# The S5 state scan, run by VectorE within the heads of the gated recurrence instead of by GpSimd beside them

## What is computed

```python
def even_mixer(h_ctx, h_lat, ...):
    u, gs, xr, gr = split_proj(h)                        # S5 input, S5 gate, recurrence input, its gate
    ys_c, ys_l = prefix_bidir(s5_scan, (grp(u_c),), (grp(u_l),), s5p(0), s5p(1))
    yr_c, yr_l = prefix_bidir(rglru_scan, (centred_dwconv(xr_c, conv_w, conv_b),),
                              (centred_dwconv(xr_l, conv_w, conv_b),), rgp(0), rgp(1))

def rglru_scan(xc, wa, ba, wx, bx, lam):
    r = sigmoid(einsum(xh, wa) + ba); ig = sigmoid(einsum(xh, wx) + bx)
    log_a = -RG_C * r * softplus(-lam)
    h[t] = exp(log_a)[t] * h[t-1] + sqrt(-expm1(2 * log_a))[t] * (ig * xf)[t]
```

## Time and profile before

| | us |
|---|---|
| median of 3 runs | 3262.89 (3262.03 to 3270.83) |
| the profiled execution | 3270.08 |
| its span, first to last instruction | 3268.5 |
| TensorE busy in the span | 2768.8 (85%) |
| VectorE busy | 1510.1 (46%) |
| ScalarE busy | 759.5 (23%) |
| GpSimd busy | 1093.3 (33%) |

### The profile page before, as it was taken

One profiled execution on the slowest core, in us unless ns is written; L12 is line 12 of the kernel. 1 busy time (PEld: TensorE's weight loads), 2 busy tenths in 40 slices (PEclk: granted clock), 3 DMA queues, 4 the chain that ended last, 5 costly groups with the idle time before them and its releaser, 6 DMA issues. The chain is left out here.

```text
span 3268.5 us, 36705 instructions
## 1 busy us (share of the span) xinstructions
PE 2768.8 (85%) x13087; PEld 2137.8 (65%) x13087; DVE 1510.1 (46%) x1800; ACT 759.5 (23%) x906; POOL 1093.3 (33%) x1187
## 2 busy tenths in 40 slices
PE   7993556898896799798996999996598888989888
PEld 6652444444443577687884788885587878878777
DVE  2207996354455222243324655555645444544611
ACT  1210222224224111222212211112223223232211
POOL 0003886888888200001112433341232313232000
PEclk8796777998998799799998999998799999999999
DMA  4510122010110655524103233333102131213332
GB/s 144 170 66 28 64 73 80 20 48 26 35 42 13 205 185 182 169 79 170 33 27 80 101 117 117 125 122 125 46 23 101 55 104 37 101 43 97 123 103 65
DMA packets 256396, 289.29 MB, mean 89 GB/s; under 512 B 34688, under 2 KB 222376, under 8 KB 255920
## 3 DMA queue, kind: packets, MB, share of 16 engines
q1 hardware_dynamic: 200800, 198.36, 19.3%
q10 hardware_dynamic: 50672, 72.89, 6.2%
q0 software_dynamic: 4832, 16.78, 1.5%
HBM read 194.70 MB, written 93.29 MB: 88 GB/s over the span
## 5 line engine op out<-in xcount | busy, mean ns | idle before, releaser
L130 PE MATMUL ps<-arena,weights 128*128 128x512 f32 (+2 forms) x2432 | 762.3, 503 | 76.9 <-ACT arena L1195 64.6
L130 PEld LDWEIGHTS ps<-arena,weights 128*128 128x128 f32 (+1 forms) x2432 | 404.7, 180 | 423.1 <-issue 323.1
L130 PE MATMUL ps<-h_part,in_weight_parts 128*128 128x512 f32 (+1 forms) x1920 | 407.8, 373 | 14.0 <-DVE h_part L1513 7.8
L130 PEld LDWEIGHTS ps<-h_part,in_weight_parts 128*128 128x128 f32 x1920 | 334.7, 189 | 81.9 <-DVE h_part L1513 9.7
L130 PE MATMUL ps<-v_part,p_part 128*128 128x512 f32 x1248 | 300.0, 400 | 0.0
L130 PE MATMUL ps<-q_part,xc_part 128*128 128x256 f32 x1920 | 252.2, 296 | 38.2 <-DVE q_part L2014 36.0
L130 PEld LDWEIGHTS ps<-q_part,xc_part 128*128 128x128 f32 x1920 | 247.8, 204 | 41.9 <-DVE q_part L2014 38.5
L130 PEld LDWEIGHTS ps<-v_part,p_part 128*128 128x128 f32 x1248 | 238.2, 193 | 49.7
L1067 PE MATMUL ps<-wo_part,mx_part 128*128 128x512 f32 x768 | 178.7, 394 | 11.3 <-DVE mx_part L1963 8.3
L2248 POOL TENSOR_TENSOR in_weight_parts<-weights,ones 128x1024 fp32r<-128x1024 f32 x32 | 77.6, 2425 | 304.7 <-PE ps L130 231.5
L1067 PEld LDWEIGHTS ps<-wo_part,mx_part 128*128 128x128 f32 x768 | 145.0, 190 | 41.9 <-issue 8.5
(11 more groups left out here) (341 smaller groups left out, 3961.2 us busy)
## 6 DMA issues: line engine op xcount, KB each, us to landing
weights<-in_e_w_in SPq DMA_DIRECT2D x32, 512.0 KB, 4.3
weights<-in_o_w_in SPq DMA_DIRECT2D x32, 512.0 KB, 4.3
arena<-in_mod_w POOLq DMA_DIRECT2D x30, 512.0 KB, 5.5
s_out_maps<-arena ACTq DMA_DIRECT2D x16, 640.0 KB, 3.0
arena<-s_out_maps SPq DMA_DIRECT2D x16, 640.0 KB, 4.5
ml_xcv<-arena ACTq DMA_DIRECT2D x16, 640.0 KB, 5.1
xm_tiles<-ml_xm SPq DMA_DIRECT2D x16, 640.0 KB, 4.1
xc_full<-ml_xcv SPq DMA_DIRECT2D x4, 2560.0 KB, 10.6
```

The source lines that it names most:

```text
L130: return nc.tensor.matmul(o, lhsT, rhs, start=(k == 0), stop=(k == n - 1))
```

## The change

The loop on GpSimd is gone. VectorE clears `WZ[:, 0]` ahead of its loop over the heads, after waiting for `wz_a`, `wz_v` and `lam_ready` as GpSimd did, and runs the same four operations a step, 40 steps a head (SH = NJ // RH), unrolled in the loop's body: 8 ahead of the first tile's convolution, 4 ahead of the second's, 12 ahead of the two L1716, and 8 at the start of each direction. As the clearing now counts up `scan` too, those who wait for the whole scan wait for 4 * NJ + 1. The semaphore `scan0` is gone.

```diff
+            V.memset(WZ[:, 0], 0.0).then_inc(sem("scan"), 1)
+            n0, per, SH = link_n[0], 17, NJ // RH
             with dve.Fori(0, RH) as i:
+                k, step = [0], [0]
+                def scan_steps(n):
+                    for j in range(step[0], step[0] + n):
+                        z = WZ[:, bass.ds(SH * i + j, 1)].rearrange("p j r g -> p (j r) g")
+                        w = WZ[:, bass.ds(SH * i + (j + 1), 1)].rearrange("p j r g -> p (j r) g")
+                        dve.wait_ge(*past("scan", 4 * SH * i + (4 * j + 1)))
+                        V.tensor_tensor(SP1, z, A1, ALU.mult).then_inc(sem("scan"), 1)
+                        V.tensor_tensor(SP2[:, ::-1], z, A2, ALU.mult).then_inc(sem("scan"), 1)
+                        dve.wait_ge(*past("scan", 4 * SH * i + (4 * j + 3)))
+                        V.tensor_tensor(SP1, SP1, SP2, ALU.add).then_inc(sem("scan"), 1)
+                        dve.wait_ge(*past("scan", 4 * SH * i + (4 * j + 4)))
+                        V.tensor_tensor(w, w, SP1, ALU.add).then_inc(sem("scan"), 1)
+                    step[0] += n
...
+                    scan_steps(8 - 4 * s)
                     dve.wait_ge(*past(f"rg_ev{s}", 6 * i + 1))
...
+                scan_steps(12)
                 for s in range(2):
                     dve.wait_ge(*past("rg_sg", 2 * i + s + 1))
                     V.tensor_tensor(SG[:, s], ps3[s], SG[:, s], ALU.mult).then_inc(sem(f"rg_ev{s}"), 1)
                 for d in range(2):
+                    scan_steps(8)
                     for s in range(2):
                         dve.wait_ge(*past(f"rg_ev{s}", 6 * i + 4 + 2 * d))
...
-            with pool.Fori(0, NJ) as i:
-                z = WZ[:, bass.ds(i, 1)].rearrange("p j r g -> p (j r) g")
-                w = WZ[:, bass.ds(i + 1, 1)].rearrange("p j r g -> p (j r) g")
-                pool.wait_ge(*past("scan", 4 * i))
-                pool.wait_ge(*past("scan0", 1))
-                GP.tensor_tensor(SP1, z, A1, ALU.mult).then_inc(sem("scan"), 1)
-                GP.tensor_tensor(SP2[:, ::-1], z, A2, ALU.mult).then_inc(sem("scan"), 1)
-                pool.wait_ge(*past("scan", 4 * i + 2))
-                GP.tensor_tensor(SP1, SP1, SP2, ALU.add).then_inc(sem("scan"), 1)
-                pool.wait_ge(*past("scan", 4 * i + 3))
-                pool.wait_ge(*past("scan0", 1))
-                GP.tensor_tensor(w, w, SP1, ALU.add).then_inc(sem("scan"), 1)
```

More of the change, by code:

```diff
@@ L94 @@
     "grow_in": ("s5_tables", 1), "fin_mm": ("pool_g", NB), "fin_sq": ("s5_in", 128), "fin_rms": ("xt_spilled", 16), "fin_y": ("xc_ready", 2 * RH),
-    "bm2": ("scan0", 1), "bn": ("u_stored0", 64), "rs": ("u_stored1", 64)}
+    "bn": ("u_stored0", 64), "rs": ("u_stored1", 64)}
 def build(nc, A, out):
@@ L1228, in _ @@
             act.wait_ge(*past("bo_stored", 16 * RH))
-            act.wait_ge(*past("scan", 4 * NJ))
+            act.wait_ge(*past("scan", 4 * NJ + 1))
             for m, name in enumerate(("ml_wq", "ml_wk", "ml_wv")):
@@ L1687, in _ @@
             dve.wait_ge(*past("e_mm1", NB // 2))
-            n0, per = link_n[0], 17
-            with dve.Fori(0, RH) as i:
-                k = [0]
+            dve.wait_ge(*past("wz_a", NB))
+            dve.wait_ge(*past("wz_v", NB))
+            dve.wait_ge(*past("lam_ready", 1))
+            V.memset(WZ[:, 0], 0.0).then_inc(sem("scan"), 1)
+            n0, per, SH = link_n[0], 17, NJ // RH
+            with dve.Fori(0, RH) as i:
+                k, step = [0], [0]
[11 more added lines that the diff above has]
+                    step[0] += n
                 def ilink(ins):
@@ L1751, in _ @@
                             V.tensor_tensor(HH[:, s], HH[:, s], SG[:, s], ALU.mult).then_inc(sem("rg_bo"), 1)
-                assert k[0] == per, k
+                assert k[0] == per and step[0] == SH, (k, step)
             link_n[0] = n0 + per * RH
             dve.wait_ge(*past("bo_stored", 16 * RH))
-            dve.wait_ge(*past("scan", 4 * NJ))
+            dve.wait_ge(*past("scan", 4 * NJ + 1))
             with dve.Fori(0, NB // 2) as i:
```

## The result

The changed kernel takes 3275.4 us (median of 9 runs, 3272.8 to 3278.2), the kernel before 3264.4 in the same comparison: ratio 1.0032, 95% interval 1.0021 to 1.0042. That is 11.1 us slower, and the interval lies clear of 1; forecast were 15.3. The profiled execution has a span of 3273.7 us, 5.2 more than that of before.

The account below looks back on a forecast made before the run. Bound: a three-engine loop per head, TensorE ending the wait before the gate products. 3 x (5.5 + 0.6 + 2.5) - 4 x 2.2 - 1.7 = +15.3 us on the 3262.9 median: 3278.2 us, range 3258 to 3300.

Parts of the forecast that it names:

- Price of a step: One scan step on VectorE, two multiplications and two sums with one address payment: 1.31 us, bounds 1.19 and 1.43.
- Directions cost nothing: Eight steps before each direction in heads 2 to 4, 10.5 us, fit VectorE's idle of 11.05 and 11.59 us.
- 24 steps in front of the gate products: Heads 2 to 4: steps before L1716 make TensorE's gate products start 5.5 us late, at 746.3 instead of 740.86.
- Code: VectorE's larger loop body leaves an instruction-fetch gap at the back edge: 0.6 us a head, bounds 0 and 3.4.
- Clock: TensorE's added idle before the gate products brings half-rate clock after it: 2.5 us a head lost, bounds 0 and 3.4.
- Port: With GpSimd quiet, VectorE's own operations shorten: 2.2 us gained a head, over four heads; bound 0.
- no relief: Rival: VectorE's operations do not shorten, with code in the open; 3306.8 us, or 3298 with cheaper steps; joint chance 0.12.
- End: Behind the last head, removing GpSimd's scan lets the state copies start earlier: 1.7 us gained at most.
- Dearer steps: Rival: address of z worked out anew, 1.43 us a step; +23.4 us, 3286.3 us; chance 0.26.
- cheap steps: Rival: address work is hidden, 1.19 us a step; +2.1 us, 3265.0 us; chance 0.14.
- code in the open: Rival part: VectorE's code fetch costs 3.4 us a head at the loop edge; up to 3306.8 us; chance 0.12 with no relief.
- The rival that the steps fit: Rival: waits on VectorE's own results cost nothing, 0.84 us a step, no loss below 1.08; 3252.4 us; chance 0.06.

Follow-up runs that it names:

- the cheaper step: Kernel after, same placement, a step's sums reordered to w = w + SP1, then w = w + SP2; 3254.1 us, ratio 0.9970 to the kernel before.

## Why the prediction was right, and by how much its terms were off

Forecast 3278.2 (3258 to 3300), measured 3275.4; slower had 0.69. The path was right: 24 steps in front of the first L1736 make TensorE wait, and the steps in the directions are covered. The sizes of the terms were less so. By its steps:

- *Price of a step.* Forecast 1.31, measured 1.32, with one address paid a step. The row of the table loop and the gap of L1711 gave it to a hundredth.
- *Directions cost nothing.* Right: VectorE still waits 4.45 and 1.12 us there. The prediction gave the waits of before as 11.05 to 11.59 us; that of head two's backward direction was 11.89, which changes nothing.
- *24 steps in front of the gate products.* From the end of a head on VectorE to the end of the first L1736 it is now 742.26 - 696.36 = 45.9 us; before, the gate products could start 740.86 - 700.76 = 40.1 us after it. So 5.8 us, forecast 5.5 and 0.6 for code. The wait that is seen on TensorE is 3.7, because VectorE's end of the head came earlier by the relief: I had said 4 to 6.
- *Code.* The gap at the loop's back edge is 0.28 us and one of 0.21 stands some steps later. 0.6 was a little too much, and no run shows the upper bound of 3.4. By the rule of the Trainium skill, Runtime: NRT & Kernel Launch, Instruction fetch mechanics, this edge would stall; the trace shows no gap over 0.28 us. That the two long operations queued at the edge hid a stall is the prediction's reading, and no run tests it.
- *Clock.* Forecast 2.5 a head from an idle of 8.2 us, measured 1.5. It was sized too high because it let up to 6.8 us at half rate fall on work; 3.3 us did. The longer idle that the figure came from is not the reason: with GpSimd kept busy TensorE idled 19.80 us, and the products behind took 27.89 us against 26.05 at the full clock, 1.8 lost.
- *Port.* Forecast 2.2 a head. From 740.86 to the end of the head's last operation it was 81.8 us before (822.6); now it is 742.26 to 822.6, 80.3 with 1.5 lost to the clock: 3.0 gained. The operations of head two, by their starts in the two traces, account for 2.9 of it: the pairs of L1730, L1747 and L1751 gained 1.5, just as forecast, L1725 and L1726 gained 0.6, and the recurrences (the old L1735, L1740 and L1744) 0.8. So what was mis-sized is the "about 0.7 more" for L1720, L1725, L1726 and the recurrences: it was 1.4, without L1720. The row that decided was L1770 with and without GpSimd; L1716, which I took as the bound for no relief, reads PSUM and never felt GpSimd.
- *End.* Forecast 1.7, measured: the last L1772 to the state copies took 1072.23 - 1065.17 = 7.1 us and takes 1080.21 - 1075.10 = 5.1, so 2.0.

The sum with the measured terms is 3 x (5.8 + 1.5) - 4 x 3.0 - 2.0 = +7.9 us, where the stage itself grew by 9.4 (from TensorE's first product of the heads, 548.55 and 547.14, to the state copies) and the medians by 11.1. So that the forecast came within 4 us of the measured change is in part luck: every term, the steps with the code included, was off towards too slow, 7.4 us in all, and 3.2 us that no term names lay the other way. Of these, 1.5 are in the stage. There TensorE's products of heads two to four lasted 6.4 us longer than before (323.3 against 316.9), and three losses of 1.5 explain 4.5; the rest is of a kind that differs from head to head in one execution too, for behind the wait between the directions, which all kernels have, the clock was granted at half for 3.5 to 6 us in the heads of the kernel before. The other 2 us, outside the stage, are not accounted for.

Dearer steps and cheap steps fall by the 1.32 us, no relief by the 1488 ns, code in the open by the gap of 0.28 us. The rival that the steps fit was decided by its threshold, which lay at 1.17 us a step rather than 1.08: it failed at 1.32 and came true at 1.11. Its mechanism, a wait that costs nothing, did not: a wait on the operation just before costs 0.11 us here. What became cheap is a wait on the operation before that one, 0.24 us from start to start where no wait at all gives 0.21, and the address work, which costs no time behind it. The sentence of the Trainium skill, VectorE: DVE Perf Modes, The DRAIN you can't avoid, that a semaphore costs nothing extra, comes near holding in this kernel for that second kind only.

## What to carry to other kernels

Idle time of an engine is worth what its pieces are worth: 62 us a head were free, and 31 us of the steps still cost time, since the idle time in front of L1716 that had to take them held only 24 x 1.08 = 26 us, and 24 x 1.17 = 28 with the relief. Put such work behind the operation that the critical engine waits for, not in front of it. Order a dependent chain so that a wait is for the operation before last where it can be, and so that an address is worked out there. With the cheaper step the same change makes the kernel 0.3% faster than before, not 0.3% slower. And when an engine is relieved, ask what it slowed: without the steps the quiet GpSimd and its earlier end made this kernel 8 us faster, and with the steps in a busy GpSimd cost 34 more.

## What the runs showed of the hardware

- A loop of four small operations on GpSimd lengthens VectorE's short ones (128x128: the second product 284 to 514 ns, the last sum only 293 to 341) and adds a tenth to most of its long ones with two SBUF inputs (the old L1730, 1488 to 1658 ns). The old L1716, with one input in PSUM, kept its 1.47 to 1.49 us. So did the convolution's L1711 its 1555 ns, in all three conditions, though both its inputs are in SBUF. Neither the kind of operation nor its scalar explains that, for the convolution's last operation is of the same kind and was slowed:

```profile
L1732 DVE SCALAR_TENSOR_TENSOR arena<-arena,param_cols x8: 1277/1278/1280, 572.9 to 976.3; 128x1024 f32<-128x1024 f32 x8
...
L1733 DVE SCALAR_TENSOR_TENSOR arena<-arena,param_cols x4: 1452/1454/1457, 716.5 to 873.7; 128x1024 f32<-128x1024 f32 x4
```

  The first line is of the kernel after, the second of the run with GpSimd kept busy. Why L1711 is spared stays open. The loss goes by operation more than by element: a step's four operations lose 0.16 us each on average, one with ten times the elements 0.17. So of what was measured here a chain of small steps beside a busy GpSimd fares worst: 1.95 us a step instead of 1.32.
- After an idle of TensorE of 1.24 us the products behind it ran at the full clock; after 3.7 us they were granted half for 3.3 us. So the last two microseconds of a wait cost more than they last: two steps moved away, 2.6 us a head, brought 4.
